# A block and two layers of a transformer on one core: the high and low parts of hT interleaved chunk by chunk

## Chip, cores and metric
The kernel runs on one core of a Trainium2 chip. The metric is the device time of one execution in microseconds; lower is better.

## What is computed
256 tokens of width 1024 go through a first block (windowed attention over several groups of heads, a gated merge of two branches, a residual) and then through two layers of a second kind. All is in fp32. Each of these layers ends in a feed-forward, which the change's title names:

```python
h = _rmsnorm(x, norm_mix[l]); z = h @ w_in[l]
# ... sparse attention, retention and convolution branches: br
proj = jnp.einsum('bsnc,ncd->bsnd', br, w_branch[l])
merged = jnp.sum(gate * proj, axis=2).astype(x.dtype)
x = x + merged @ w_out[l]
h2 = _rmsnorm(x, norm_mlp[l])
x = x + jnp.square(jax.nn.relu(h2 @ w_ff1[l])) @ w_ff2[l]   # 1024 -> 4096 -> 1024
```

## The kernel before
TensorE gets fp32 products from operands in the type fp32r. Each operand is split into a high part (rounded to fp32r) and a low part (the rest), and a product is three matmuls: high by high, high weights' part by low, low by high. The weights stream from memory into slots of `ring`, half a weight panel at a time; ScalarE rounds them to their high part (line 596), VectorE subtracts to get the low part (line 630), both into `ring_parts`.

The activations stand transposed in `hT`: 128 partitions, then high and low part, then `KC` = 8 chunks of 128 features, then `TOKENS` = 256 tokens. So the high parts of all chunks lie together, 2048 numbers per partition, and the low parts follow. `hT_hi` and `hT_lo` are the two halves. Who uses them:
- `rows_out` (lines 921 and 925) takes 128 tokens of a chunk of `hT` as the stationary operand and streams 512 columns of weights from `ring_parts` past it. This is the bulk of the products.
- `columns_out` (lines 967 to 969) does it the other way round for four narrow panels of a layer: the weights are stationary, and the 256 tokens of one chunk of `hT_hi` or `hT_lo` stream.
- `wide_columns_out` does the feed-forward's first product. At line 992 the high part of the weights is stationary, and the 256 high and the 256 low numbers of a chunk stream past it in one matmul of 512 columns: two runs of 256 numbers that lie 2048 apart. The two results stand side by side in a PSUM bank. At line 995 the low part of the weights meets the 256 high numbers. A layer has 16 panels of 128 x 2 columns; each group of 128 columns is eight matmuls of line 992 and then eight of line 995 (in the first panel pair, four and four, twice).

`hT` is written from PSUM tiles that hold transposed rows: ScalarE writes the high part (lines 1453, 1617, 1768, and 1477 at the start), VectorE subtracts it and writes the low part (`low_tile` at line 1889, and lines 1853, 1899, 2098, 2479). A tile is 4 chunks of one block of 128 tokens. In the first block the tokens stand in another order while the attention runs; `sorted_columns` gives the places in hT for them, so there a tile's 128 tokens go to 64 pairs of neighbouring columns, every second pair. Before the change VectorE does such a tile in one instruction of line 1889.

The order of the work is written out by hand. Around these evictions it is: PE multiplies the last branch (`br11`), transposes the merged rows of chunks 0 to 3 (line 1006, `tok`) between two of its matmuls, and waits in `columns_ready` for both blocks of these chunks before `wo0` begins; the same again for chunks 4 to 7, in the middle of `wo0`. `merged_low` calls `low_tile` for block 0 and block 1 in turn.

Of the kernel before, what the change touches and what calls it, by code (L numbers as in the profile page):

```python
# [31 lines left out]
F32R = mybir.dt.float32r  # L32
ALU = mybir.AluOpType
# [3 lines left out]
P = 128  # L37
TOKENS, D = 256, 1024
NB = TOKENS // P
KC = D // P  # L40
# [301 lines left out]
def block_kernel(nc, a, out):  # L342

    ctx = ExitStack()
    with ctx:
        def sb(name, *shape):
            return ctx.enter_context(nc.sbuf_tensor(name, [P, *shape], F32))
# [4 lines left out]
        def both_types(name, *shape):  # L352

            offset = -(-nc.sbuf_base // 32) * 32
            whole = sb(name, *shape)
            return whole, nc.alloc_sbuf_tensor_at(f"{name}_parts", [P, *shape], F32R, offset=offset)

        ring, ring_lo = both_types("ring", SLOTS + HI_SLOTS, HALF)
        hT = ctx.enter_context(nc.sbuf_tensor("hT", [P, 2, KC, TOKENS], F32R))
        hT_hi, hT_lo = hT[:, 0], hT[:, 1]  # L360
        x = sb("x", NB, D)
        tok = sb("tok", NB, D)
        ident = sb("ident", P)
# [174 lines left out]
        def layer(l):  # L538
            return Part(TILES_2, PANELS_2, HALVES_2, HIGH_2, LAYER_HALVES, l)
# [113 lines left out]
        def sorted_columns(t, i, b):  # L653

            return t[:, 4 * i:4 * i + 4, :].rearrange("p k (i b s) -> p k b i s", b=NB, s=2)[:, :, b]
# [14 lines left out]
        def hidden_parts():  # L670

            return [parts(AREA_2["ffT"], 8192 * i, 8192).rearrange("p (k t) -> p k t", k=32) for i in range(2)]

        def tile_of(eng, part, name):
            return tile[wait_done(eng, tile_done, part, "tile", name)]

        def panel_of(eng, part, name):
            return panel[wait_done(eng, panel_done, part, "panel", name)]

        def tile_sem(part, name):  # L680
            return tile_evicted[part.turn("tile", name)[0]]
# [179 lines left out]
        def _(pe):  # L861
            def tile_for(part, name):

                b, before = part.turn("tile", name)
                if part.l is not None or before:
                    pe.wait_ge(tile_evicted[b], before)
                return tile[b], tile_done[b]

            def panel_for(part, name):

                b, before = part.turn("panel", name)
                if part.l is not None or before:
                    pe.wait_ge(panel_evicted[b], before * 2)
                return panel[b], panel_done[b]
# [14 lines left out]
            def wait_parts(part, name):  # L889

                if part.l is not None and name in BY_TRANSFER:
                    slot = part.turn("half", name)[0]
                    pe.wait_ge(low_added[slot], 16 * (part.l * len(TRANSFERS[slot]) + TRANSFERS[slot].index(name) + 1))
                else:
                    pe.wait_ge(low_ready, lows_by_vector(part, index_of(part, name)))
                return parts_of(part, name)
# [75 lines left out]
            def wide_columns_out(part, i, groups=1, before_last=None, after={}):  # L972

                n = KC // groups
                for group in range(groups):
                    if group:
                        before_last()
                    for j in range(2):  # L980
                        name = f"ff{i}{j}"
                        if group == 0:
                            ps, done = panel_for(part, name)
                        else:
                            b, _ = part.turn("panel", name)
                            ps, done = panel[b], panel_done[b]
                        hi, lo = (w.rearrange("p (k n) -> p k n", k=KC) for w in wait_parts(part, f"ff{i}/{j}"))
                        for m in range(2):
                            cols = slice(m * P, (m + 1) * P)
                            chunks = range(n * group, n * group + n)  # L990
                            for k in chunks:
                                pe.matmul(ps[:, m, :].rearrange("p (s t) -> p s t", s=2), hi[:, k, cols], hT[:, :, k, :], start=(k == 0),  # L992
                                          stop=(k == KC - 1), skip_group_check=True)
                            for k in chunks:
                                mm = pe.matmul(ps[:, m, 0:TOKENS], lo[:, k, cols], hT_hi[:, k, :], start=False, stop=(k == KC - 1),  # L995
                                               skip_group_check=True)
                            if group == 0 and 2 * j + m in after:
                                after[2 * j + m]()
                        if group == groups - 1:
                            mm.then_inc(done, 1)  # L1000
# [46 lines left out]
            part = part_1  # L1047
# [178 lines left out]
            for l in range(LAYERS):  # L1226
                part = layer(l)
# [3 lines left out]
                ps, done = tile_for(part, "rs")  # L1231
# [200 lines left out]

                columns_ready(part, "z", 0)
                wide_columns_out(part, 0, 2, lambda: columns_ready(part, "z", 1), {b: lambda b=b: turn_last(b) for b in range(NB)})
                for i in range(1, FF_PANELS):
                    wide_columns_out(part, i)
# [387 lines left out]
        def _(v):  # L1824
            part = part_1
# [6 lines left out]
            for c in (8, 10):  # L1832
                e = v.tensor_scalar(first[:, c:c + 1], first[:, c:c + 1], HD ** -0.5, None, ALU.mult)
# [47 lines left out]
            def low_tile(part, name, i, b, scale):  # L1881

                ps = tile_of(v, part, f"{name}{b}{i}")
                ks, bs = slice(4 * i, 4 * i + 4), slice(b * P, (b + 1) * P)
                if part.l is None:
                    lo, of, hi = sorted_columns(hT_lo, i, b), ps[:, :].rearrange("p (c i s) -> p c i s", c=4, s=2), sorted_columns(hT_hi, i, b)
                else:
                    lo, of, hi = hT_lo[:, ks, bs], ps[:, :].rearrange("p (c t) -> p c t", c=4), hT_hi[:, ks, bs]
                v.scalar_tensor_tensor(lo, of, scale, hi, ALU.mult, ALU.subtract).then_inc(tile_sem(part, f"{name}{b}{i}"), 1)

            def merged_low(part, i, base):

                for b in range(NB):
                    v.wait_ge(merged_high, base + (2 * i + b + 1))
                    low_tile(part, "m", i, b, 0.5)
# [258 lines left out]
            for l in range(LAYERS):  # L2154
                part = layer(l)
# [11 lines left out]
                ps = panel_of(v, part, "gr")  # L2167
# [11 lines left out]
                ps = panel_of(v, part, "cb")  # L2179
                for b in range(NB):  # L2180
                    e = v.tensor_tensor(tz2[:, b], ps[:, b, :].rearrange("p (c t) -> p c t", c=2), R2, ALU.mult)
# [8 lines left out]
                ps = panel_of(v, part, "ca")  # L2190
# [21 lines left out]
                ps = panel_of(v, part, "k4")  # L2212
# [3 lines left out]
                for i in range(2):  # L2216
                    for g in range(2):
                        s = i * TOKENS
                        rows = slice(HD * g, HD * g + HD)
                        v.tensor_tensor(kcP[0:HD, i, g, :], ps[rows, 0, s:s + TOKENS], R[rows, :], ALU.mult)  # L2220
                        e = v.tensor_tensor(kcP[HD:P, i, g, 0:TOKENS - 1], ps[rows, 0, s + 1:s + TOKENS], R[rows, 1:TOKENS], ALU.mult)
# [6 lines left out]
                for i in range(2):  # L2228
                    for g in range(2):

                        lo = kcP[:, i, g, :].rearrange("p (n j s) -> p j n s", j=8, s=2)
                        for half in range(2):
                            src = lo[:, :, half:half + N_CMP, 0]
                            e = v.tensor_tensor(blk[:, i, 8 * half:8 * half + 8, g * N_CMP:(g + 1) * N_CMP], src,
                                                pe_[:, i, 8 * half:8 * half + 8].unsqueeze(2).broadcast_to([P, 8, N_CMP]), ALU.add)
# [8 lines left out]
                ps = panel_of(v, part, "q")  # L2244
# [228 lines left out]
                for b in range(NB):  # L2473
                    ps = tile_of(v, part, f"z{b}1")
                    bs = slice(b * P, (b + 1) * P)
                    v.wait_ge(z_high, l * NB + b + 1)
                    for c in range(4):
                        k = 4 + c
                        e = v.scalar_tensor_tensor(hT_lo[:, k, bs], ps[:, c * P:(c + 1) * P], gains[:, k:k + 1], hT_hi[:, k, bs],
                                                   ALU.mult, ALU.subtract)  # L2480
# [3 lines left out]
                hi, lo = hidden_parts()  # L2484
# [281 lines left out]
```

## Time and profile before

| | us |
|---|---|
| median of three timed runs | 1155.58 |
| lowest, highest | 1155.33, 1157.27 |
| profiled execution | 1155.98 |
| its span | 1154.2 |
| TensorE busy | 1139.2 (99%) |
| VectorE busy | 823.8 (71%) |
| ScalarE busy | 586.8 (51%) |

The rows further down come from the profiled execution. PE are matmuls, PEld loads of their stationary operand, DVE is VectorE, ACT ScalarE. A matmul's duration runs from its start until its last result is out, and the next one starts long before that; how fast they follow each other is read from the starts.

### The profile page before, as it was taken

To read this page: it belongs to the slowest core of one execution; us is meant where nothing else is said; L and a number is where in the kernel's file an instruction comes from. 1 tells how busy PE (TensorE), PEld (TensorE's weight loads), DVE (VectorE), ACT (ScalarE), POOL (GpSimd) and SP (SyncE) were. 2 spreads that over 40 slices of the span, in tenths; PEclk is the share of its full clock that TensorE was granted. 3 is DMA by queue.
4 is the path that set the end of the run, shared out by engine and by line. 5 is a ranking of instruction groups with operands and counts; after the bars stand their busy time and mean duration, and the time that the engine had idled before them with its cause. 6 is when DMAs were issued, how large, how long until landed. Compare 5 with 4: busy or idle time off the path is not lost.

```text
span 1154.2 us, 15957 instructions
## 1 busy us (share of the span) xinstructions
PE 1139.2 (99%) x6207; PEld 949.7 (82%) x6207; DVE 823.8 (71%) x1245; ACT 586.8 (51%) x736; POOL 137.2 (12%) x152
## 2 busy tenths in 40 slices
PE   8999999999999999999999999999999999999997
PEld 6888777787998777888888888998777878888886
DVE  5565656666689899787777454599899787777443
ACT  6445565643426666634555333525776534555332
POOL 1222231100003143000000000003234000000000
PEclk9999999999999999999999999999999999999999
DMA  9556543457545668654555555545678654555640
GB/s 359 199 182 209 190 176 130 172 189 267 181 150 202 202 183 223 199 194 150 187 195 196 206 189 194 172 153 215 187 214 221 182 182 150 215 183 186 218 161 37
DMA packets 35323, 219.34 MB, mean 190 GB/s; under 512 B 3888, under 2 KB 5680, under 8 KB 10928
## 3 DMA queue, kind: packets, MB, share of 16 engines
q1 hardware_dynamic: 32800, 204.67, 50.7%
q0 software_dynamic: 1728, 12.58, 5.8%
q8 instruction: 50, 0.82, 0.3%
q10 hardware_dynamic: 720, 1.06, 0.3%
q14 instruction: 25, 0.20, 0.1%
HBM read 217.25 MB, written 1.05 MB: 189 GB/s over the span
## 4 chain that ended last, share of the span: by engine, by line
PE 81%; issue 15%; DVE 1%; ACT 1%; DVEq 1%; DMA 0%; POOL 0%; POOLq 0%; ACTq 0%
PE panel L921 35%; PE panel L925 17%; PE panel L992 5%; PE tile L1006 4%; PE panel L995 3%; PE panel L969 3%; PE panel L968 3%; PE panel L967 3%; PE heads_out L1346 1%; PE heads_out L1200 1%; PE tile L1260 1%; PE tile L1369 1%; PE tile L1366 1%; DVEq L2058 1%; DMA area<-in_x_columns_dram 0%
## 5 line engine op out<-in xcount | busy, mean ns | idle before, releaser
L630 DVE TENSOR_TENSOR ring_parts<-ring,ring_parts 128x2048 fp32r<-128x2048 f32 (+2 forms) x172 | 389.8, 2271 | 160.3 <-ACT ring_parts L596 154.4
L596 ACT ACTIVATE ring_parts<-ring 128x2048 fp32r<-128x2048 f32 (+2 forms) x184 | 346.9, 1888 | 253.4 <-PE panel L925 202.0
L921 PE MATMUL panel<-ring_parts,hT 128*128 128x512 f32 (+2 forms) x1344 | 327.6, 390 | 3.4 <-issue 2.1
L921 PEld LDWEIGHTS panel<-ring_parts,hT 128*128 128x128 f32 x1344 | 240.0, 188 | 59.3 <-issue 12.2
L921 PE MATMUL panel<-ring_parts,area_parts 128*128 128x512 f32 x736 | 177.4, 389 | 0.0
L925 PE MATMUL panel<-ring_parts,hT 128*128 128x512 f32 (+2 forms) x672 | 170.4, 388 | 0.0
L921 PEld LDWEIGHTS panel<-ring_parts,area_parts 128*128 128x128 f32 x736 | 137.9, 188 | 28.5
L925 PEld LDWEIGHTS panel<-ring_parts,hT 128*128 128x128 f32 x672 | 121.2, 188 | 25.5 <-issue 2.5
L992 PE MATMUL panel<-hT,ring_parts 128*128 128x512 f32 x512 | 129.9, 393 | 0.0
L2205 DVE SCALAR_TENSOR_TENSOR area<-area,cw 128x256 f32<-128x256 f32 x240 | 104.8, 498 | 2.8
L992 PEld LDWEIGHTS panel<-hT,ring_parts 128*128 128x128 f32 x512 | 91.6, 189 | 16.0
L925 PE MATMUL panel<-ring_parts,area_parts 128*128 128x512 f32 x376 | 93.7, 390 | 0.0
L925 PEld LDWEIGHTS panel<-ring_parts,area_parts 128*128 128x128 f32 x376 | 70.4, 188 | 14.5
L995 PEld LDWEIGHTS panel<-hT,ring_parts 128*128 128x128 f32 x512 | 70.9, 190 | 5.7
L995 PE MATMUL panel<-hT,ring_parts 128*128 128x256 f32 x512 | 72.6, 282 | 0.0
L967 PE MATMUL panel<-hT,ring_parts 128*128 128x256 f32 x256 | 72.6, 284 | 0.0
L969 PE MATMUL panel<-hT,ring_parts 128*128 128x256 f32 x256 | 72.5, 283 | 0.0
L968 PE MATMUL panel<-hT,ring_parts 128*128 128x256 f32 x256 | 72.4, 283 | 0.0
L1782 ACT ACTIVATE area<-panel 128x512 f32<-128x512 f32 x32 | 19.1, 598 | 77.8 <-PE panel L995 77.8
L2538 POOL TENSOR_SCALAR stat<-stat 128x16 f32<-128x16 f32 (+2 forms) x13 | 2.6, 201 | 469.7 <-ACT area L1463 246.1
L967 PEld LDWEIGHTS panel<-hT,ring_parts 128*128 128x128 f32 x256 | 49.1, 192 | 0.0
L968 PEld LDWEIGHTS panel<-hT,ring_parts 128*128 128x128 f32 x256 | 49.1, 192 | 0.0
(248 smaller groups left out, 1135.9 us busy)
## 6 DMA issues: line engine op xcount, KB each, us to landing
ring<-in_w_layers_dram SPq DMA_DIRECT2D x140, 1024.0 KB, 4.9
ring<-in_w_first_dram SPq DMA_DIRECT2D x38, 1024.0 KB, 5.0
ring_parts<-in_w_layers_dram POOLq DMA_DIRECT2D x12, 1024.0 KB, 8.7
ring<-in_w_first_dram SPq DMA_DIRECT2D x5, 512.0 KB, 10.4
area<-in_second_bias_dram SPq DMA_DIRECT2D x8, 320.0 KB, 3.1
ring<-in_w_layers_dram SPq DMA_DIRECT2D x4, 560.0 KB, 4.0
area<-in_first_bias_dram SPq DMA_DIRECT2D x4, 384.0 KB, 4.3
area<-in_later_bias_dram SPq DMA_DIRECT2D x1, 1536.0 KB, 12.2
```

Of the source, the lines that this page charges most:

```text
L596: act.activation(ring_lo[:, SLOTS + hi, 0:w], ring[:, slot, 0:w], ACT.Copy).then_inc(high_ready, 1)
L630: g.tensor_tensor(ring_lo[:, slot, 0:w], ring[:, slot, 0:w], ring_lo[:, SLOTS + hi, 0:w], ALU.subtract).then_inc(low_ready, 1)
L921: pe.matmul(ps[:, b, 0:width], t[:, 4 * i + k, b * P:(b + 1) * P], hi[:, k, :], start=(i == k == 0 and t is of[0]), stop=False)
L925: return pe.matmul(ps[:, b, 0:width], of[0][:, 4 * i + k, b * P:(b + 1) * P], lo[:, k, :], start=False, stop=(i == len(halves) - 1 and k = ...
L967: pe.matmul(to, hi[:, k, cols], hT_hi[:, k, :], start=(k == 0), stop=False)
L968: pe.matmul(to, hi[:, k, cols], hT_lo[:, k, :], start=False, stop=False)
L969: mm = pe.matmul(to, lo[:, k, cols], hT_hi[:, k, :], start=False, stop=(k == KC - 1))
L992: pe.matmul(ps[:, m, :].rearrange("p (s t) -> p s t", s=2), hi[:, k, cols], hT[:, :, k, :], start=(k == 0), stop=(k == KC - 1), skip_group ...
L995: mm = pe.matmul(ps[:, m, 0:TOKENS], lo[:, k, cols], hT_hi[:, k, :], start=False, stop=(k == KC - 1), skip_group_check=True)
L1006: mm = pe.transpose(ps[0:rows, i * P:(i + 1) * P], source(i), ident[:, :])
L1782: act.activation(sq[:, i % 2, j * 512:(j + 1) * 512].rearrange("p (m t) -> p m t", m=2), ps[:, :, TOKENS:2 * TOKENS], ACT.Copy).then_inc(c ...
L2205: v.scalar_tensor_tensor(acc[:, c, :], src, cw[:, c, j:j + 1], acc[:, c, :], ALU.mult, ALU.add)
```

## The change
`hT` gets the order chunk, part, token. High and low numbers of a chunk then lie side by side, 512 in a row, and line 992 streams them as one run. `hT_hi` and `hT_lo` become views with a step of 512 numbers from chunk to chunk instead of 256.

```diff
-        hT = ctx.enter_context(nc.sbuf_tensor("hT", [P, 2, KC, TOKENS], F32R))
-        hT_hi, hT_lo = hT[:, 0], hT[:, 1]
+        hT = ctx.enter_context(nc.sbuf_tensor("hT", [P, KC, 2, TOKENS], F32R))
+        hT_hi, hT_lo = hT[:, :, 0], hT[:, :, 1]
...
-                                pe.matmul(ps[:, m, :].rearrange("p (s t) -> p s t", s=2), hi[:, k, cols], hT[:, :, k, :], start=(k == 0),
+                                pe.matmul(ps[:, m, :], hi[:, k, cols], hT[:, k].rearrange("p s t -> p (s t)"), start=(k == 0),
                                           stop=(k == KC - 1), skip_group_check=True)
...
                 if part.l is None:
-                    lo, of, hi = sorted_columns(hT_lo, i, b), ps[:, :].rearrange("p (c i s) -> p c i s", c=4, s=2), sorted_columns(hT_hi, i, b)
-                else:
-                    lo, of, hi = hT_lo[:, ks, bs], ps[:, :].rearrange("p (c t) -> p c t", c=4), hT_hi[:, ks, bs]
+                    of = ps[:, :].rearrange("p (c i s) -> p s c i", c=4, s=2)
+                    lo, hi = (sorted_columns(t, i, b).rearrange("p c i s -> p s c i") for t in (hT_lo, hT_hi))
+                    for s in range(2):
+                        e = v.scalar_tensor_tensor(lo[:, s], of[:, s], scale, hi[:, s], ALU.mult, ALU.subtract)
+                    e.then_inc(tile_sem(part, f"{name}{b}{i}"), 1)
+                    return
+                lo, of, hi = hT_lo[:, ks, bs], ps[:, :].rearrange("p (c t) -> p c t", c=4), hT_hi[:, ks, bs]
                 v.scalar_tensor_tensor(lo, of, scale, hi, ALU.mult, ALU.subtract).then_inc(tile_sem(part, f"{name}{b}{i}"), 1)
```

The pairs of the first block are the reason for the second part: with 256 numbers from chunk to chunk the pairs of all four chunks formed one regular row (256 pairs, four numbers apart), with 512 they don't, and VectorE's instruction has one dimension too few for chunk, pair and number in the pair. So it is given twice, once for the first and once for the second number of every pair.

On VectorE, in the first block around the evictions of the merged columns, there stands before:

```order
211 L2061 TENSOR_TENSOR tok<-tok,area 128x512 x2
212 L1889 SCALAR_TENSOR_TENSOR hT<-tile,hT 128x256x2 x2
213 L630 TENSOR_TENSOR ring_parts<-ring,ring_parts 128x2048
214 L2055 SCALAR_TENSOR_TENSOR area<-area,panel 128x512 x2
215 L2061 TENSOR_TENSOR tok<-tok,area 128x512 x2
216 L1889 SCALAR_TENSOR_TENSOR hT<-tile,hT 128x256x2 x2
```

And now, where lines 2059 and 2065 are the old 2055 and 2061:

```order
211 L2065 TENSOR_TENSOR tok<-tok,area 128x512 x2
212 L1889 SCALAR_TENSOR_TENSOR hT<-tile,hT 128x4x64 x4
213 L630 TENSOR_TENSOR ring_parts<-ring,ring_parts 128x2048
214 L2059 SCALAR_TENSOR_TENSOR area<-area,panel 128x512 x2
215 L2065 TENSOR_TENSOR tok<-tok,area 128x512 x2
216 L1889 SCALAR_TENSOR_TENSOR hT<-tile,hT 128x4x64 x4
```

Nothing has moved; at both places two instructions of 512 numbers have become four of 256. On ScalarE, at the same point, the high part's evictions (line 1617) stay as many, in another shape. Before:

```order
116 L596 ACTIVATE ring_parts<-ring 128x2048 x4
117 L1617 ACTIVATE hT<-tile 128x256x2 x2
118 L596 ACTIVATE ring_parts<-ring 128x2048
119 L1617 ACTIVATE hT<-tile 128x256x2 x2
120 L596 ACTIVATE ring_parts<-ring 128x2048 x3
```

And now:

```order
116 L596 ACTIVATE ring_parts<-ring 128x2048 x4
117 L1617 ACTIVATE hT<-tile 128x4x64x2 x2
118 L596 ACTIVATE ring_parts<-ring 128x2048
119 L1617 ACTIVATE hT<-tile 128x4x64x2 x2
120 L596 ACTIVATE ring_parts<-ring 128x2048 x3
```

The order on PE, GpSimd and SyncE is the same in both kernels, row for row.

## Rows read from the trace of the kernel before

**Rows 1.** The page: busy time by engine, the granted clock by slice.
```profile
PE 1139.2 (99%) x6207; PEld 949.7 (82%) x6207; DVE 823.8 (71%) x1245; ACT 586.8 (51%) x736; POOL 137.2 (12%) x152
...
PEclk9999999999999999999999999999999999999999
```

**Rows 2.** Timeline, PE, feed-forward: start us, length of the merged row us, line, count.
```profile
561.03 2.00 PE L992 MATMUL panel<-hT,ring_parts 128*128 128x512 f32 x8
562.88 1.11 PE L995 MATMUL panel<-hT,ring_parts 128*128 128x256 f32 x8
563.83 2.00 PE L992 MATMUL panel<-hT,ring_parts 128*128 128x512 f32 x8
...
622.49 2.00 PE L992 MATMUL panel<-hT,ring_parts 128*128 128x512 f32 x8
```

**Rows 3.** Timeline, PE, behind the feed-forward's first product: first and last of five rows.
```profile
630.87 3.82 PE L921 MATMUL panel<-ring_parts,area_parts 128*128 128x512 f32 x16
...
641.77 1.52 PE L921 MATMUL panel<-ring_parts,area_parts 128*128 128x512 f32 x6
```

**Rows 4.** Timeline, PE, two runs behind four transposes.
```profile
543.83 0.60 PE L1006 MATMUL tile<-ident,x 128*128 128x128 f32 x4
544.18 1.17 PE L992 MATMUL panel<-hT,ring_parts 128*128 128x512 f32 x4
545.19 0.63 PE L995 MATMUL panel<-hT,ring_parts 128*128 128x256 f32 x4
```

**Rows 5.** Timeline, PE, one run behind four transposes.
```profile
285.99 0.60 PE L1006 MATMUL tile<-ident,tok 128*128 128x128 f32 x4
286.34 1.17 PE L921 MATMUL panel<-ring_parts,hT 128*128 128x512 f32 x4
287.35 0.85 PE L925 MATMUL panel<-ring_parts,hT 128*128 128x512 f32 x3
```

**Rows 6.** Timeline in narrow windows, PE: what runs at 41.6, and from 43.61 on.
```profile
41.28 0.70 PE L921 MATMUL panel<-ring_parts,hT 128*128 128x512 f32 x2
...
43.45 1.75 PE L921 MATMUL panel<-ring_parts,hT 128*128 128x512 f32 x7
```

**Rows 7.** Timeline, PE, narrow panels: first and last of 84 starts.
```profile
302.03 0.29 PE L969 MATMUL panel<-hT,ring_parts 128*128 128x256 f32 x1
...
311.99 0.28 PE L968 MATMUL panel<-hT,ring_parts 128*128 128x256 f32 x1
```

**Rows 8.** Line 1889 alone: duration ns min/median/max, first and last start us.
```profile
L1889 DVE SCALAR_TENSOR_TENSOR hT<-tile,hT x12: 680/686/693, 262.9 to 952.2; 128x512 fp32r<-128x512 f32 x12
```

**Rows 9.** Timeline, first block's merged columns; in brackets idle before and who ended it.
```profile
262.92 1.29 DVE L1889 SCALAR_TENSOR_TENSOR hT<-tile,hT 128x512 fp32r<-128x512 f32 x2 [2.51 <-ACT hT L1617]
...
264.13 2.28 DVE L630 TENSOR_TENSOR ring_parts<-ring,ring_parts 128x2048 fp32r<-128x2048 f32 x1
...
264.47 3.91 PE L921 MATMUL panel<-ring_parts,hT 128*128 128x512 f32 x16 [0.41 <-DVE hT L1889]
...
268.21 0.61 PE L925 MATMUL panel<-ring_parts,hT 128*128 128x512 f32 x2
...
269.05 1.09 PE L1006 MATMUL tile<-ident,tok 128*128 128x128 f32 x8 [0.22 <-DVE tok L2061]
...
270.40 1.29 DVE L1889 SCALAR_TENSOR_TENSOR hT<-tile,hT 128x512 fp32r<-128x512 f32 x2 [1.41 <-ACT hT L1617]
...
271.80 0.94 PE L921 MATMUL panel<-ring_parts,hT 128*128 128x512 f32 x3 [0.25 <-issue]
```

**Rows 10.** Timeline, VectorE, contiguous evictions of 256 and 128 numbers.
```profile
400.13 0.42 DVE L2352 TENSOR_TENSOR area<-tile,decay 128x256 f32<-128x256 f32 x1
400.46 0.28 DVE L2353 TENSOR_TENSOR area<-tile,decay 128x128 f32<-128x128 f32 x1
```

**Rows 11.** Two lines with a stepped input on VectorE: duration ns min/median/max.
```profile
L2234 DVE TENSOR_TENSOR area<-area,par x16: 330/350/359, 343.5 to 775.1; 128x120 f32<-128x120 f32 x16
...
L2319 DVE TENSOR_TENSOR area<-tile,area x4: 345/351/357, 398.4 to 828.3; 128x120 f32<-128x120 f32 x4
```

## Prediction

> **What bounds the kernel now.** I read the page first. TensorE is busy 99% of the span, and the granted clock is at its upper level, 2.4 GHz, in all 40 slices [rows 1]. So a microsecond is won only by matmuls that follow each other faster, or by a wait of PE that goes. VectorE is busy 71% and does not bound as a whole; it counts only where PE waits for it. "Busy" says nothing of the rate, because matmuls overlap. What counts is the distance from start to start, which the timeline gives.
>
> The wide products are line 992, 512 of them over two layers. In steady state eight of them alternate with eight products of line 995. From start to start, eight of line 992 take 562.88 - 561.03 = 1.85 us, 231 ns each; eight of line 995 take 563.83 - 562.88 = 0.95 us, 119 ns each [rows 2]. The neighbours that already read one run of 512 numbers are lines 921 and 925: right behind the feed-forward's first product they do 48 from 630.87 to 641.77 (16, 8, 16 and 8), 227 ns each [rows 3]. So there are 4 ns between them, and the question is whether the two runs make them.
>
> **Part 1: the wide products read one run.** Three comparisons say that the two runs cost nothing or nearly so.
> First, the surplus stands only behind short matmuls. Lines 992 and 921 both occur four at a time right behind four transposes. Line 992: from 544.18 to 545.19, 1.01 us. Line 921, with one run: from 286.34 to 287.35, again 1.01 us [rows 4, 5]. Same number of columns, same neighbours ahead, same time.
> Second, a longer stretch of line 921, behind eight transposes: the first product starts at 41.28 and its successor is over at 41.98; at some 0.39 us each that one started at 41.59. The tenth of the 16 starts at 43.45 (seven are left from there). These eight distances are 1.86 us, 232 ns each, with one run of 512 numbers [rows 6]; the two runs behind eight short products need 1.85. So what line 992 has above 227 ns is what any 512-column product has in its first steps behind short ones.
> Third, the bound. From 561.03 to 622.49 there are 22 groups of eight and eight, 2.794 us each [rows 2]. With 8 x 0.227 = 1.817 us (48 in 10.90 us) for the wide ones, and eight of 256 columns at the 120 ns that lines 967 to 969 keep up (83 steps from 302.03 to 311.99, each with one run [rows 7]), a group would take 2.777. The surplus is 0.017 us per group, and there are 512/8 = 64 groups: 1.1 us if all of it came from the two runs. A loss is excluded, since the new pattern is the very one that line 921 has. The term lies between -1.1 and 0 us; I take 0, by the two comparisons behind short matmuls. Weight loads read the ring, not hT, and do not change.
>
> **Part 2: the other readers and writers of hT.** Lines 921 and 925 load their weights from a run of 128 numbers of hT, and lines 967 to 969 and 995 stream one run of 256; before and after these runs are whole, only the step from chunk to chunk changes. VectorE and ScalarE write in runs of 128 or 256 numbers, four runs at double the step, or whole chunks. I cost all of this at nothing: the twelve evictions of line 1889, eight of which write four runs of 128 and four of which write pairs, all take 680 to 693 ns [rows 8]. ScalarE's eviction of the first block's merged columns (line 1617) keeps its pairs of neighbouring numbers; its pattern only can't be folded any more. It stays one instruction.
>
> **Part 3: VectorE's eviction of the low part in the first block.** This is what really changes. Before, line 1889 did one tile with one instruction of 512 numbers; now it takes two of 256, one for the even and one for the odd columns of each pair. Four instructions become eight, and each reads PSUM at every second number and reads and writes hT at every fourth.
> Who waits: PE begins wo0 only when both blocks of chunks 0 to 3 are evicted. VectorE starts at 262.92 and ends the pair at 264.21; PE, idle for 0.41 us on exactly this, starts at 264.47. The same happens for chunks 4 to 7: 270.40 to 271.69, and PE starts at 271.80 [rows 9]. No work covers these two places, so every nanosecond of the eviction is a nanosecond of PE. In the layers line 1889 keeps its form.
> What queues behind: the low part of the next half (line 630, 264.13 to 266.41) is wanted by PE at 268.21 [rows 9]. PE is delayed as much as it is, so its slack of 1.8 us stays. VectorE works on without a gap until PE's next wait for it, 0.22 us before 269.05 [rows 9]; that stays as it is, since both slip together.
> The price from below, no cost for the steps: two instructions of 512 numbers take 1.29 us together [rows 9]. A contiguous one of 256 numbers out of PSUM lasts 0.42 us and lets the next start after 0.33 us (400.13 to 400.46) [rows 10]. Four of them: 3 x 0.33 + 0.42 = 1.41 us, 0.12 more than now. Two places: +0.3 us.
> The price with steps: the trace has two like operations, of 120 numbers each. Line 2234 reads its first input at every 16th number, line 2319 its second, backwards, also at every 16th, and its first from PSUM in one run. They last 350 and 351 ns [rows 11]. A contiguous one of 128 numbers lasts 0.28 us [rows 10], with 8 fewer at some 1 ns each 0.27. So the step costs 0.08 us over 120 numbers, 0.65 ns each, whichever operand is stepped. On 256 numbers that is 0.17 us: a half would start its successor after 0.50 us and last 0.59. Four: 3 x 0.50 + 0.59 = 2.09 us, 0.80 more than now; two places: +1.6 us.
> The upper end: three stepped operands, and should each add its own 0.17 us, the next half starts after 0.84 us, four take 3 x 0.84 + 0.92 = 3.44, and the two places cost +4.3 us.
> I take +1.6, since both stepped rows of this engine show the price and nothing shows that it adds up.
> The Trainium skill has a rule that speaks here. "Advanced Engine Details and Errata", section "Memory Cachelines", says that SBUF is read in lines of 16 bytes and that an access which meets a new line each time is penalised. Worked out for this case: a step of four fp32 numbers is just such a case, where the old pairs met each line twice. By it the price is there at a step of four as at one of 16, with no figure. "VectorE: DVE Perf Modes", section "The TRN2 errata", gives (N + 151)/0.96 ns for such an operation, with no term for steps: 424 ns, my lower case. The row of line 2234 (350 ns, where that formula gives 282) departs from it [rows 11].
>
> **Sum.** Profiled run 1155.98 us (span 1154.2, 1.8 around it) + 0 + 0 + 1.6 = 1157.6. This execution lies 0.4 above the median of the three timed runs, 1155.58; against the median the time is 1157.2.
>
> **The rivals.**
> Free steps: line 1889's halves run as contiguous ones. For it: writes in runs of 2 of every 4 numbers cost nothing now [rows 8]. Against it: lines 2234 and 2319. Then +0.3: 1155.9.
> Steps that add up: one mechanism, at the two waits of PE for line 1889, which ends on the other side. With a distance s from half to half the two places cost 8 s - 2.4 us (s + 0.09 being the length of the last). The loss passes 2.3 us from s = 0.59 us; I forecast 0.50. At 0.84 it is +4.3: 1159.9, slower. For it: PSUM and both uses of hT are stepped at once, in the two lines with a step only one operand is [rows 11]. Against it: whether a read from one side or the other was stepped made no difference there, so they seem to run side by side.
> The two runs did cost: the full surplus goes, -1.1, with free steps: -0.8, 1154.8. With my price of the steps it is +0.5. For it: the 4 ns of line 992. Against it: the same distances on line 921 behind short matmuls.
>
> **How the numbers follow.** My forecast 0.45, at 1157.2. Free steps 0.31, 1155.9. Adding steps 0.15, 1159.9. Costly runs 0.07, 1154.8 to 1156.1. Something unseen that wins 0.2% or more, 0.02. About 0.2% (2.3 us) is what a measurement of this kernel can tell from no change, so "same" is 1153.3 to 1157.9. Slower: the adding steps, and a tenth of my own case: 0.19. Faster: 0.02. Same: 0.79. The range goes from 1154.4, just below where the costly runs end, to 1158.9, which takes in my case with the 1.7 us by which the highest of the three timed runs, 1157.27, lies above their median, and a part of the adding steps; some 0.15 is left out above and 0.04 below.
>
> **What the profile after would show.** Part 1: eight wide products still 1.85 us from start to start, and 1.01 behind four transposes. If they take 1.82 or less the two runs did cost. Part 3: eight instructions at line 1889 in the first block, about 0.59 us each; PE's start of wo0 0.8 us later than now, its next 1.6 later, and the same 1.6 at every point behind, to the end. Halves of 0.42 us mean free steps; of 0.9 us, adding ones. I am wrong in kind if PE's waits there don't grow with the eviction, or if the feed-forward stretch changes its length by more than 0.7 us per layer.

## The result

| | before | after |
|---|---|---|
| median of 22 timed runs, us | 1156.67 | 1158.89 |
| lowest, highest | 1155.33, 1157.63 | 1157.38, 1159.57 |
| span of the profiled execution, us | 1154.2 | 1155.8 |

The ratio is 1.0017, with a 95% interval of 1.0010 to 1.0023: a small loss, 1.2 to 2.7 us, and clear of zero. The 22 runs of the kernel before have a median 1.1 us above that of the three shown ahead, so the absolute time is higher than those three let one expect. The times of both kernels fall into a lower and an upper group some 1.3 us apart (10 and 12 runs before, 6 and 16 after), and within a group the kernel after is 1.7 to 1.9 us slower, so that the 2.2 us between the two medians are in part the unequal shares of the groups.

The page and the timeline of PE in the feed-forward of the kernel after:

```profile
PE 1139.2 (99%) x6207; PEld 949.6 (82%) x6207; DVE 825.4 (71%) x1249; ACT 586.7 (51%) x736; POOL 137.2 (12%) x152
```
```profile
557.01 2.00 PE L992 MATMUL panel<-hT,ring_parts 128*128 128x512 f32 x8
558.85 1.11 PE L995 MATMUL panel<-hT,ring_parts 128*128 128x256 f32 x8
559.80 2.00 PE L992 MATMUL panel<-hT,ring_parts 128*128 128x512 f32 x8
...
629.64 2.00 PE L992 MATMUL panel<-hT,ring_parts 128*128 128x512 f32 x8
```

Eight wide products take 558.85 - 557.01 = 1.84 us from start to start, eight of line 995 0.95, and the 26 groups from 557.01 to 629.64 take 2.793 us each, against 2.794 before [rows 2]. PE is busy for the same 1139.2 us. The run of 512 numbers has won nothing that these rows show.

VectorE has four instructions more (1249 against 1245) and is busy for 1.6 us more. Where they lie, line 1889 alone (duration in ns, first and last start) and then the timeline:

```profile
L1889 DVE SCALAR_TENSOR_TENSOR hT<-tile,hT x8: 597/626/657, 262.7 to 272.7; 128x256 fp32r<-128x256 f32 x8
```
```profile
261.44 1.03 PE L1006 MATMUL tile<-ident,tok 128*128 128x128 f32 x8
...
262.73 2.22 DVE L1889 SCALAR_TENSOR_TENSOR hT<-tile,hT 128x256 fp32r<-128x256 f32 x4 [2.51 <-ACT hT L1617]
...
264.84 2.31 DVE L630 TENSOR_TENSOR ring_parts<-ring,ring_parts 128x2048 fp32r<-128x2048 f32 x1
...
265.21 3.89 PE L921 MATMUL panel<-ring_parts,hT 128*128 128x512 f32 x16 [1.34 <-DVE hT L1889]
...
269.78 1.09 PE L1006 MATMUL tile<-ident,tok 128*128 128x128 f32 x8 [0.23 <-DVE tok L2065]
...
271.13 2.19 DVE L1889 SCALAR_TENSOR_TENSOR hT<-tile,hT 128x256 fp32r<-128x256 f32 x4 [1.41 <-ACT hT L1617]
...
273.42 3.89 PE L921 MATMUL panel<-ring_parts,hT 128*128 128x512 f32 x16 [1.16 <-issue]
```

The eviction of two tiles takes 2.22 and 2.19 us where it took 1.29 and 1.29 [rows 9]. PE's wait grows from 0.41 to 1.34 us at the first place and from 0.25 to 1.16 at the second: 0.93 + 0.91 = 1.84 us. The wait for line 2065 (2061 before) stays at 0.23 us. This is the whole of the loss: from PE's start of wo0's second half to the end it is 1154.2 - 271.80 = 882.4 us before and 1155.8 - 273.42 = 882.4 after, with both layers and their feed-forwards in it. The spans differ by 1.6 since this execution of the kernel after got to the first place 0.2 us earlier.

In what follows a place is measured within one execution, so that its start does not matter: from the eight transposes (line 1006) to PE's start of wo0. In the timeline of the kernel before they stand just ahead of [rows 9]:

```profile
261.63 1.03 PE L1006 MATMUL tile<-ident,tok 128*128 128x128 f32 x8
```

This gives 264.47 - 261.63 = 2.84 us before and 265.21 - 261.44 = 3.77 after; and from there to the start of wo0's second half, 271.80 - 264.47 = 7.33 before and 273.42 - 265.21 = 8.21 after.

### The profile page after: what moved, and what is told of

Read it like the earlier page. It is cut to its first block, busy times and chain, and to the rows that moved or that the text cites. A ratio compares the mean times of both kernels' runs of the same rounds, so it can differ in the third digit from the quotient of the medians.

```text
span 1155.8 us, 15961 instructions
## 1 busy us (share of the span) xinstructions
PE 1139.2 (99%) x6207; PEld 949.6 (82%) x6207; DVE 825.4 (71%) x1249; ACT 586.7 (51%) x736; POOL 137.2 (12%) x152
## 4 chain that ended last, share of the span: by engine, by line
PE 81%; issue 15%; DVE 1%; ACT 1%; POOL 0%; DMA 0%; DVEq 0%; POOLq 0%; ACTq 0%
PE panel L921 35%; PE panel L925 17%; PE panel L992 5%; PE tile L1006 4%; PE panel L995 3%; PE panel L969 3%; PE panel L968 3%; PE panel L967 3%; PE heads_out L1346 1%; PE heads_out L1200 1%; PE tile L1260 1%; PE tile L1369 1%; PE tile L1366 1%; DMA area<-in_x_columns_dram 0%; PE panel L1077 0%
```

## Is it the eviction, and is the new layout worth nothing by itself?

Two kernels take the change apart. The first keeps the old layout and has only the eviction in even and odd columns:

```diff
                 if part.l is None:
-                    lo, of, hi = sorted_columns(hT_lo, i, b), ps[:, :].rearrange("p (c i s) -> p c i s", c=4, s=2), sorted_columns(hT_hi, i, b)
+                    of = ps[:, :].rearrange("p (c i s) -> p s c i", c=4, s=2)
+                    lo, hi = (sorted_columns(t, i, b).rearrange("p c i s -> p s c i") for t in (hT_lo, hT_hi))
+                    for s in range(2):
+                        e = v.scalar_tensor_tensor(lo[:, s], of[:, s], scale, hi[:, s], ALU.mult, ALU.subtract)
```

> The old layout of hT with line 992 untouched (two runs of 256), and only line 1889 in the first block split into even and odd columns, as in the changed kernel. Theory (the loss is the eviction, the run of 512 is worth nothing): eight halves of about 0.6 us, 2.2 us for four where the two old ones took 1.29, PE's starts of wo0 and of its second half 0.9 and 1.8 us later, the whole about 1.0017 of before, the same as the changed kernel. Rival (the one run of 512 did win up to 1.1 us and hides part of a larger loss): 1.0025 or more.

The second has the new layout with one instruction per tile. It leaves out the factor 0.5 on the first block's merged rows, so it doesn't compute the same:

```diff
-                    for s in range(2):
-                        e = v.scalar_tensor_tensor(lo[:, s], of[:, s], scale, hi[:, s], ALU.mult, ALU.subtract)
+                    e = v.tensor_tensor(lo, of, hi, ALU.subtract)
...
-                    act.activation(to, of, ACT.Copy, scale=0.5).then_inc(merged_high, 1)
+                    act.activation(to, of, ACT.Copy, scale=1.0 if part.l is None else 0.5).then_inc(merged_high, 1)
```

> The new layout with line 992 on one run, and the low part evicted with one plain subtraction per tile, an instruction that has room for three dimensions. The factor 0.5 on the first block's merged rows is left out for it (the high part is taken with factor 1), so this part of the computation differs; all else is as in the changed kernel. Theory: 0.69 us each, 1.29 for two, PE's starts there as in the old kernel, ratio 1.0000 within 0.0006, so the layout alone moves nothing. Rival (the run of 512 wins up to 1.1 us): 0.999.

Old layout, split eviction: 1.0015 of the kernel before (1.0006 to 1.0024). Its timeline:

```profile
261.90 1.04 PE L1006 MATMUL tile<-ident,tok 128*128 128x128 f32 x8
...
263.19 2.18 DVE L1889 SCALAR_TENSOR_TENSOR hT<-tile,hT 128x256 fp32r<-128x256 f32 x4 [2.51 <-ACT hT L1617]
265.63 3.91 PE L921 MATMUL panel<-ring_parts,hT 128*128 128x512 f32 x16 [1.31 <-DVE hT L1889]
```

New layout, one instruction: 0.9994 (0.9986 to 1.0003). Its timeline:

```profile
261.86 1.04 PE L1006 MATMUL tile<-ident,tok 128*128 128x128 f32 x8
...
263.15 1.29 DVE L1887 TENSOR_TENSOR hT<-tile,hT 128x512 fp32r<-128x512 f32 x2 [2.51 <-ACT hT L1617]
264.70 3.91 PE L921 MATMUL panel<-ring_parts,hT 128*128 128x512 f32 x16 [0.41 <-DVE hT L1887]
```

The old layout with the split has 3.73 us from the transposes to wo0 (+0.89 on 2.84); the new layout without it has 2.84, with the wait of 0.41 us unchanged. So the loss moves with the eviction and not with the layout. The layout alone is within what the runs can tell, and its interval still admits the -1.1 us that the prediction had as its bound; the start-to-start distances in the kernel after, equal to those before to 1 ns a group, are the sharper evidence, and they say 0. So does the stretch from wo0's second half to the end, in these two kernels as well: 882.35 us in the old layout, 882.39 in the new. The two kernels of the next section take 882.35 in the old layout and 882.70 in the new, so no kernel of the new layout is shorter there.

## Is it the number of instructions, or the steps?

The split brings two things at once: twice the instructions, and operands read and written at every 2nd or 4th number. One kernel keeps the old layout and splits each tile into two halves of two chunks, whose pairs stay pairs. The other has the new layout and four instructions a tile, one for each chunk, in pairs too:

```diff
+                    for h in range(2):
+                        cs = slice(2 * h, 2 * h + 2)
+                        e = v.scalar_tensor_tensor(lo[:, cs], of[:, cs], scale, hi[:, cs], ALU.mult, ALU.subtract)
```

> The old layout and line 992 untouched; line 1889 in the first block split in two halves of two chunks each, which keep their pairs of neighbouring numbers: the same number of instructions and of numbers as in the changed kernel, without the steps. Theory (the steps make most of the loss): 0.42 us each, four take 1.41 us, +0.12 at each place, +0.25 us in all, ratio 1.0002. Rival (two instructions instead of one make it): 0.6 us each and ratio 1.0017, as with the steps.

```diff
+                    for c in range(4):
+                        e = v.scalar_tensor_tensor(lo[:, c], of[:, c], scale, hi[:, c], ALU.mult, ALU.subtract)
```

> The new layout with line 992 on one run, and the first block's low part evicted chunk by chunk: four instructions of 128 numbers in pairs for a tile, 16 in all, no step beyond the pairs. Theory: each lasts 0.28 us and lets the next start after 0.20, eight take 7 x 0.20 + 0.28 = 1.68 us against 1.29 in the old kernel and 2.2 in the changed one: +0.4 at each place, +0.8 us in all, ratio 1.0007. Rival (the cost is per instruction, not per step): eight instructions cost more than four, above +0.9 at each place, ratio 1.002 or more.

Halves in pairs, old layout: 1.0000 (0.9992 to 1.0009).

```profile
263.24 1.04 PE L1006 MATMUL tile<-ident,tok 128*128 128x128 f32 x8
...
264.53 1.42 DVE L1889 SCALAR_TENSOR_TENSOR hT<-tile,hT 128x256 fp32r<-128x256 f32 x4 [2.51 <-ACT hT L1617]
266.20 3.92 PE L921 MATMUL panel<-ring_parts,hT 128*128 128x512 f32 x16 [0.54 <-DVE hT L1889]
```

Chunk by chunk, new layout: 1.0006 (0.9997 to 1.0015).

```profile
262.27 1.04 PE L1006 MATMUL tile<-ident,tok 128*128 128x128 f32 x8
...
263.56 1.67 DVE L1888 SCALAR_TENSOR_TENSOR hT<-tile,hT 128x128 fp32r<-128x128 f32 x8 [2.51 <-ACT hT L1617]
265.49 3.89 PE L921 MATMUL panel<-ring_parts,hT 128*128 128x512 f32 x16 [0.80 <-DVE hT L1888]
```

Four halves in pairs take 1.42 us, four stepped ones 2.18 to 2.22: of the 0.93 us more at the first place, 0.13 are the extra instructions and 0.8 the steps. Eight instructions of 128 numbers still take only 1.67 us. From the transposes to wo0 it is 2.96 and 3.22 us, so +0.12 and +0.38, as expected. Both timed ratios can't be told from 1, but they stand in the order of the waits.

## Which operand's step costs?

In this kernel, on the old layout, each tile has its own operand stepped: the PSUM input by 2 in the first, the input from hT by 4 in the second, the output into hT by 4 in the third, nothing in the fourth. The numbers combined are then not the right ones.

> The old layout; line 1889 in the first block in two halves of 256 numbers for each of the four tiles, and one operand stepped in each tile: the PSUM input at every 2nd number (first tile), the input from hT at every 4th (second), the output into hT at every 4th (third), none (fourth). The numbers that are combined are then not the right ones in the first three tiles. Forecast's picture (any one stepped operand costs 0.17 us on 256 numbers, and several together no more): 0.59 us for halves of the first three tiles, 0.42 for the fourth. Rival a (only the SBUF side pays, every access meeting a new 16-byte line): 0.42 for the first and fourth, 0.59 for the second and third. Rival b (the shares add up): each of the three less than 0.17 above the fourth, 0.19 in sum.

Seven of the eight instructions, in order (two of each tile, and the first of the fourth), from narrow windows of VectorE's timeline:

```profile
262.90 0.43 DVE L1901 SCALAR_TENSOR_TENSOR hT<-tile,hT 128x256 fp32r<-128x256 f32 x1 [2.51 <-ACT hT L1617]
...
263.24 0.41 DVE L1901 SCALAR_TENSOR_TENSOR hT<-tile,hT 128x256 fp32r<-128x256 f32 x1
...
263.57 0.60 DVE L1901 SCALAR_TENSOR_TENSOR hT<-tile,hT 128x256 fp32r<-128x256 f32 x1
...
264.09 0.61 DVE L1901 SCALAR_TENSOR_TENSOR hT<-tile,hT 128x256 fp32r<-128x256 f32 x1
...
270.89 0.62 DVE L1901 SCALAR_TENSOR_TENSOR hT<-tile,hT 128x256 fp32r<-128x256 f32 x1 [1.41 <-ACT hT L1617]
...
271.36 0.62 DVE L1901 SCALAR_TENSOR_TENSOR hT<-tile,hT 128x256 fp32r<-128x256 f32 x1
...
271.82 0.41 DVE L1901 SCALAR_TENSOR_TENSOR hT<-tile,hT 128x256 fp32r<-128x256 f32 x1
```

The PSUM input at every second number is free: 0.43 and 0.41 us, as in the fourth tile. A read from hT at every fourth number makes 0.60 us, and the next may start after 0.52; a write at every fourth number makes 0.62, and the next starts after 0.47. All three together, in the kernel after, are 0.60 to 0.66 long and 0.51 to 0.54 apart. So the shares don't add up, and the rows are those that rival a forecast. That it is the memory which decides is not shown by them, because the PSUM input was stepped by 2 and the operands in hT, which lies in SBUF, by 4.

Does every second number cost too? The same kernel with steps of 2 on the hT side (nothing in the first tile, input in the second, output in the third and fourth):

> The old layout; line 1889 in the first block in two halves for each of the four tiles. First tile: nothing stepped, 0.42 us. Second tile: the input from hT at every 2nd number (8 bytes). Third and fourth: the output into hT at every 2nd number, nothing else. The numbers that are combined are then not the right ones. Reading at every 4th number had taken 0.61 us and writing at every 4th 0.62. Theory by lines of 16 bytes (two numbers of each line are used, as with the pairs that cost nothing): 0.42 us in all tiles. Rival (numbers are moved in pairs, and a lone number costs a pair's time): 0.6 us for the second to fourth tile, as with a step of 4.

```profile
L1899 DVE SCALAR_TENSOR_TENSOR hT<-tile,hT x8: 415/416/425, 263.3 to 271.9; 128x256 fp32r<-128x256 f32 x8
```

All eight take 415 to 425 ns. For operands in SBUF a step of 2 is free on VectorE, for reads and writes; a step of 4 is not. So the size of the step decides there, and since a step of 2 is free in both memories, no run tells them apart: a PSUM input at a step of 4 was not tried. The Trainium skill's rule for SBUF, "Advanced Engine Details and Errata", "Memory Cachelines" (lines of 16 bytes, and at least two hits on a line to hide the access latency), fits the rows in hT of both kernels; it gives no figure.

## When does a pattern cost TensorE anything?

The wide products lost nothing by two runs. Does their pattern matter at all? Panels 2 to 7 of the feed-forward read 512 numbers of hT in other patterns; the feed-forward then computes with other numbers than it should.

```diff
+                                if i >= 2:
+                                    f = (2, 4, 8)[i // 2 - 1]
+                                    flat = hT[:, :, :, :].rearrange("p s k t -> p (s k t)")
+                                    at = k // f * 512 * f
+                                    of, to = flat[:, at:at + 512 * f].rearrange("p (n f) -> p f n", f=f)[:, k % f], ps[:, m, :]
```

> The old kernel, with the moving operand of line 992 read otherwise in three quarters of the panels: panels 0 and 1 as before (two runs of 256), panels 2 and 3 at every 2nd number of hT, 4 and 5 at every 4th, 6 and 7 at every 8th, always 512 numbers. The feed-forward then gets other numbers than it should. Theory from the profile (TensorE takes its moving operand at the same pace whatever the pattern, so two runs could cost nothing): 1.85 us for eight in all panels and no change of the total. Rival (a pattern that meets a new 16-byte line with each number costs, as on VectorE by about 0.6 ns a number, and two runs meet as few new lines as one): steps of 4 and 8 slower, up to 0.3 us more per product, 2.4 us more for eight; step 2 in between or free.

PE's timeline; line 998 is the wide product here. First two runs of 256, then steps of 2, 4 and 8:

```profile
560.89 2.00 PE L998 MATMUL panel<-hT,ring_parts 128*128 128x512 f32 x8
562.74 1.12 PE L1001 MATMUL panel<-hT,ring_parts 128*128 128x256 f32 x8
563.69 3.77 PE L998 MATMUL panel<-hT,ring_parts 128*128 128x512 f32 x8
567.28 1.14 PE L1001 MATMUL panel<-hT,ring_parts 128*128 128x256 f32 x8
...
600.22 3.85 PE L998 MATMUL panel<-hT,ring_parts 128*128 128x512 f32 x8
603.89 1.14 PE L1001 MATMUL panel<-hT,ring_parts 128*128 128x256 f32 x8
...
637.39 3.61 PE L998 MATMUL panel<-hT,ring_parts 128*128 128x512 f32 x8
640.83 1.13 PE L1001 MATMUL panel<-hT,ring_parts 128*128 128x256 f32 x8
```

Eight take 1.85 us, then 3.59, 3.67 and 3.44: 231 ns each against 449, 459 and 430. The theory that TensorE takes any pattern at one pace has fallen. The whole is 1239.6 us, 82.7 above a run of the kernel before taken with it (1156.88); 128 products of each kind make 128 x (218 + 228 + 199) ns = 82.6. And the step of 2, free on VectorE, costs TensorE as much as a step of 4. So a second kernel looked for the run length at which it ends: runs of 2 that start every 4 numbers, of 4 every 8, of 32 every 64.

> The old kernel, with the moving operand of line 992 read in short runs in three quarters of the panels: panels 0 and 1 as before (two runs of 256), panels 2 and 3 in runs of 2 numbers that start every 4, panels 4 and 5 in runs of 4 that start every 8, panels 6 and 7 in runs of 32 that start every 64; always 512 numbers. The feed-forward gets other numbers than it should. Every 2nd, 4th and 8th number alone had cost 449, 459 and 430 ns a product against 231. Theory now (TensorE takes its moving numbers two at a time, and only a pair that is torn costs): 231 ns for all, whatever the run's length. Rival a (each run's start costs a little, so two runs would be nearly but not quite free): 2 and 4 visibly above 231, 32 near it. Rival b (lines of 16 bytes count): runs of 2 cost about half of what single numbers do, runs of 4 nothing.

```profile
564.37 3.77 PE L997 MATMUL panel<-hT,ring_parts 128*128 128x512 f32 x8
567.97 1.14 PE L1000 MATMUL panel<-hT,ring_parts 128*128 128x256 f32 x8
...
600.91 2.03 PE L997 MATMUL panel<-hT,ring_parts 128*128 128x512 f32 x8
602.78 1.11 PE L1000 MATMUL panel<-hT,ring_parts 128*128 128x256 f32 x8
...
623.47 2.06 PE L997 MATMUL panel<-hT,ring_parts 128*128 128x512 f32 x8
625.36 1.11 PE L1000 MATMUL panel<-hT,ring_parts 128*128 128x256 f32 x8
```

Runs of 2: 3.60 us for eight, 450 ns each. Runs of 4: 1.87, 234 ns. Runs of 32: 1.89, 236 ns. The theory that only torn pairs cost has fallen as well, since whole pairs cost the full price, and rival b was right on the runs of 4 and wrong on half the price for 2. Rival a (a price for each run's start) doesn't fit either: there are eight times as many starts with runs of 4 as with runs of 32, and they are no slower. What the rows show: where each four numbers (16 bytes, counted from the start of hT) are used whole, the pace is within 3% of that of two runs of 256; where only one or two of the four are used, a product takes about twice as long. The Trainium skill's rule on lines holds here only in part: runs of 2 hit each line twice and yet cost the full price, so for TensorE the measurement decides. Two runs of 256 are far on the free side, so joining them had nothing to win. Why runs of 32 are a little slower than runs of 4 stays open, as does a run of 4 that is not aligned.

## Can the wait be covered?

What both kernels show is that PE waits for the eviction of chunks 0 to 3 with nothing beside it, in the first block and (at 515.98, 0.40 us) in the layers. The transposes ahead of it can come one quarter earlier:

```diff
-                rows_out(part, branch, of, [f"{branch}/0"], after={2: lambda: turn_columns(part, "m", tok, 0, merged, base)})
+                rows_out(part, branch, of, [f"{branch}/0"], after={1: lambda: turn_columns(part, "m", tok, 0, merged, base)})
```

> The old kernel, right in all it computes, with the transposes of merged chunks 0 to 3 one quarter earlier in the last branch's product (four 512-column products earlier), in the first block and both layers. What the case showed is that PE waits for the eviction behind these transposes with nothing to cover it, 0.41 us in the first block and 0.40 in each layer. Theory: VectorE's rows for them are ready at 260.41, so the transposes can start at 260.7; the eviction then ends 0.9 us earlier relative to PE, and the three waits of 0.4 us go: -1.2 us, ratio 0.999. Rival: the transposes now wait for VectorE's line 2061, or the low part of wo0's weights comes late behind the earlier eviction, and the wait only moves: ratio 1.0000 or above.

On the old kernel: 0.9991 (0.9982 to 1.0000), span 1152.7 us.

```profile
260.28 1.09 PE L1006 MATMUL tile<-ident,tok 128*128 128x128 f32 x8
...
263.96 3.79 PE L921 MATMUL panel<-ring_parts,hT 128*128 128x512 f32 x16
...
266.41 1.29 DVE L2061 TENSOR_TENSOR tok<-tok,area 128x512 f32<-128x512 f32 x2
...
268.05 1.03 PE L1006 MATMUL tile<-ident,tok 128*128 128x128 f32 x8
...
270.74 2.55 PE L921 MATMUL panel<-ring_parts,hT 128*128 128x512 f32 x10 [0.28 <-issue]
...
511.52 1.09 PE L1006 MATMUL tile<-ident,tok 128*128 128x128 f32 x8 [0.66 <-DVE tok L2061]
```

In the first block the wait is gone, and the 0.22 us before the next transposes too. In the layers the rival holds: the wait of 0.40 us for the eviction and the next one of 0.24 for line 2061 are gone, but the earlier transposes now wait 0.66 us for their rows from line 2061. From the start of wo0's second half in the first block to the end it is 1152.7 - 270.74 = 882.0 us against 882.4, so both layers together gave 0.4 us and not the 0.8 of the theory. The rest of the 1.5 us by which the span is shorter was won, or arrived early (some 0.2 us), by 270.74. The timed gain is about 0.1%, with an interval that just reaches no change. This kernel has the lowest median of the kernels that compute everything. The same edit on the changed kernel asks whether its longer eviction can hide:

> The changed kernel with the transposes of merged chunks 0 to 3 one quarter earlier, as in the run on the old kernel just before, where PE began wo0 1.0 us after the eviction had ended. Theory (the eviction's extra length counts only where nothing covers it): at the first place the 0.93 us more of line 1889 fit into that 1.0 us and vanish, at the second (chunks 4 to 7, not moved) the 0.9 us stay. So this kernel's span is 1.4 us (the gain of the move in the old one, 0.4 to 0.5 for each of three places) and about 0.9 us below the changed kernel's 1155.8, some 1153.5; ratio to before 0.9994 to 1.0000. Rival (VectorE's work behind the eviction, line 630 and the rows for the next transposes, carries the delay on to the next wait of PE): the 0.93 us come back at PE's wait for line 2061's rows, span 1154.4, ratio 1.0002 to 1.0006.

Measured: 1.0001 (0.9992 to 1.0010), span 1154.5 us.

```profile
260.51 1.09 PE L1006 MATMUL tile<-ident,tok 128*128 128x128 f32 x8
...
261.86 2.18 DVE L1889 SCALAR_TENSOR_TENSOR hT<-tile,hT 128x256 fp32r<-128x256 f32 x4 [1.41 <-ACT hT L1617]
...
264.30 3.91 PE L921 MATMUL panel<-ring_parts,hT 128*128 128x512 f32 x16
...
267.52 1.29 DVE L2065 TENSOR_TENSOR tok<-tok,area 128x512 f32<-128x512 f32 x2
...
268.87 1.09 PE L1006 MATMUL tile<-ident,tok 128*128 128x128 f32 x8 [0.22 <-DVE tok L2065]
...
272.52 3.67 PE L921 MATMUL panel<-ring_parts,hT 128*128 128x512 f32 x15 [1.16 <-issue]
```

PE starts wo0 almost unhindered, 264.30 - 260.51 = 3.79 us after the transposes against 263.96 - 260.28 = 3.68 on the old kernel. But VectorE has no gap between the eviction and line 2065, so that it ends 8.30 us after those transposes (268.81 - 260.51) instead of 7.42 (267.70 - 260.28), 0.88 later, and PE now waits there: 268.87 - 264.30 = 4.57 us from wo0 to the next transposes against 268.05 - 263.96 = 4.09. Of 0.9 us, 0.11 + 0.48 = 0.6 us came back. The theory that the slack in front of wo0 hides it has fallen, and the rival holds, for two thirds of the amount: in this stretch VectorE's chain itself is near the critical path. The second place costs its 0.9 us as before: 272.52 - 268.87 = 3.65 us from the transposes to wo0's second half, against 270.74 - 268.05 = 2.69 on the old kernel.

## Why the prediction was right

- Part 1, 0 us: right. The distances of the wide products are the same to 1 ns, and the two comparisons with line 921 behind short matmuls were what told it; the 4 ns of difference to steady 227 ns had suggested a gain of up to 1.1 us.
- Part 2, nothing: right; the new layout with one instruction leaves the waits as they were.
- Part 3, the place: right. Both waits of PE took the whole extra length of the eviction, line 630 and line 2061 slipped with PE, and nothing was absorbed later.
- Part 3, the size: +1.6 forecast, 1.84 measured. The mis-sized term is the half: 0.50 us apart and 0.59 long forecast, 0.51 to 0.54 and 0.60 to 0.66 measured. That it came out so near was helped by luck: the price was read from steps of 16 and used for a step of 4, and a step of 2 would have been free. "Whichever operand is stepped" went further than its rows: in both lines of rows 11 the stepped operand lies in SBUF, so they say nothing of PSUM. That costs don't add up was right.
- The formula (N + 151)/0.96 ns is stated in the Trainium skill, "VectorE: DVE Perf Modes", "The TRN2 errata", for an fp32 addition by tensor_tensor, checked at 512 and 2048 numbers; the estimate of 424 ns from it is near the 415 to 425 that scalar_tensor_tensor took on 256 numbers without a costly step.
- The level, 1157.2 against 1158.89: 1.1 us of the 1.7 is the level of the kernel before, whose three first runs lay low, and 0.6 the loss, 2.2 by the medians for 1.6 forecast; the interval of the ratio is 1.5 us wide. The range ended at 1158.9, 0.01 us above the measured time; that the time lies within it is luck, and what bears the forecast out is the two waits.
- Free steps, adding steps and costly runs are each excluded by a run of their own or by the distances above.

## What to carry to other kernels

Before joining two runs of an operand, compare start-to-start distances with a product that already has one run and the same kind of neighbours; steady products make a short-lived surplus behind short ones look like a cost of the pattern. A layout for one engine is paid for by all that write it: look for evictions whose dimensions can no longer be folded, and let TensorE use every four neighbouring fp32 numbers whole and VectorE at least two of every four in SBUF. Where an engine waits for an eviction with nothing beside it, each nanosecond there counts once for every such place, and moving work ahead helps only until the next item in the evicting engine's chain is the late one.

## What the runs showed that I had not expected

- A moving operand of fp32r numbers with a step of 2, 4 or 8 numbers takes 430 to 459 ns for 512 columns instead of 231, and whole pairs at every second pair 450 ns, but whole fours 234 ns.
- A step of 2 fp32 numbers is free on VectorE in SBUF (read and write) and in PSUM (read), 415 to 426 ns for 256 numbers; a step of 4 in SBUF makes it 600 to 620 ns, and read and write together cost no more than the read alone, within 0.05 us. A step of 4 in PSUM was not run.
